# A hybrid inference step: weights of the first projection by column, top-k over halves, attention's units in another order

## What is computed

```python
def reference(...):
    for layer in range(2):
        mp = split(silu(c_ctx) @ mod_w[layer] + mod_b[layer], 6)     # context
        ms = split(silu(c) @ mod_w[layer] + mod_b[layer], 6)         # latent
        hp, hs = modulate(xp, norm1_g, mp[0], mp[1]), modulate(xs, norm1_g, ms[0], ms[1])
        if layer == 0:   # gate, u = x @ w_in; conv over 4; h_t = a_t h_(t-1) + b_t, both ways
            yp, ys = recurrent_mixer(hp, ...), recurrent_mixer(hs, ...)   # (h * gelu(gate)) @ w_out
        else:            # 16 heads of 64, 4 of keys; window of 128; sink; context keys for all
            yp, ys = context_attention(...) @ w_o, latent_attention(...) @ w_o
        xp, xs = xp + mp[2] * yp, xs + ms[2] * ys
        xp = xp + mp[5] * experts(modulate(xp, norm2_g, mp[3], mp[4]))
        xs = xs + ms[5] * experts(modulate(xs, norm2_g, ms[3], ms[4]))

def experts(x):
    aff = softmax(x @ w_router)                     # tokens x 16
    g, idx = top_k(aff.T, cap)                      # per expert, cap = tokens / 8
    h = silu(x[idx] @ w_gate) * (x[idx] @ w_up)
    return zeros.at[idx].add((h @ w_down) * g)
```

## Time and profile before

| | |
|---|---|
| median of 3 runs | 1864.85 us (1864.16 to 1870.14) |
| the profiled execution | 1864.11 us, its span 1862.3 us |
| PE busy | 1659.7 us, 89% of the span |
| DVE, ACT, POOL busy | 614.3, 370.4, 312.1 us |
| HBM read | 500.50 MB |

### The profile page before, as it was taken

The page is one execution under the profiler, slowest core; times in us unless marked ns, Lnnn a source line. Parts: engine busy times, 40 slices in busy tenths (PEclk is TensorE's granted clock), DMA queues, the critical chain, the costliest instruction groups (busy, mean ns, idle before and its releaser), DMA issues.

```text
span 1862.3 us, 30729 instructions
## 1 busy us (share of the span) xinstructions
PE 1659.7 (89%) x13351; PEld 771.2 (41%) x13351; DVE 614.3 (33%) x1137; ACT 370.4 (20%) x770; POOL 312.1 (17%) x358
## 2 busy tenths in 40 slices
PE   4799859479999999999879788794799999999997
PEld 0688647123333333332258666472233333333322
DVE  2467675510111121010267567556101111210102
ACT  2377741100000000000151355411000000000000
POOL 1133230210101110110020167301101011101110
PEclk8899979689999999999989899896899999999999
DMA  9400553989999999999920200315899999999993
GB/s 390 146 1 1 214 224 119 410 335 404 382 405 410 399 407 414 401 404 405 336 85 1 96 24 24 137 79 216 313 405 381 403 410 399 405 415 398 407 356 115
DMA packets 57934, 524.99 MB, mean 282 GB/s; under 512 B 12607, under 2 KB 12895, under 8 KB 25038
## 3 DMA queue, kind: packets, MB, share of 16 engines
q1 hardware_dynamic: 48096, 490.62, 64.9%
q0 software_dynamic: 8176, 27.08, 5.2%
q10 hardware_dynamic: 1534, 5.38, 0.7%
HBM read 500.50 MB, written 22.55 MB: 281 GB/s over the span
## 4 chain that ended last, share of the span: by engine, by line
PE 77%; DVE 9%; DMA 5%; ACT 5%; issue 2%; POOL 1%; SPq 0%; DVEq 0%; POOLq 0%; ACTq 0%
PE ps L912 36%; PE ps L916 18%; PE ps L855 6%; PE ps L1170 5%; DMA W<-x_hat,gi_c 2%; DMA ring<-in_mod_w 2%; DMA ring<-in_rg_w_in 1%; PE ps L1218 1%; PE ps L1192 1%; PE ps L1205 1%; PE ps L939 1%; PE ps L1077 1%; PE ps L954 1%; PE ps L759 1%; ACT W L1426 1%
## 5 line engine op out<-in xcount | busy, mean ns | idle before, releaser
L912 PE MATMUL ps<-ring,W 128*32 128x512 f32 x4608 | 552.4, 597 | 4.0 <-issue 2.6
L916 PE MATMUL ps<-ring,W 128*16 128x512 f32 x2304 | 300.2, 593 | 0.0
L912 PEld LDWEIGHTS ps<-ring,W 128*32 128x32 f32 x4608 | 145.9, 110 | 335.1 <-issue 333.0
L1241 ACT ACTIVATE W<-ps 128x512 f32<-128x512 f32 (+5 forms) x137 | 72.0, 542 | 910.5 <-PE ps L954 707.7
L1738 DVE TENSOR_TENSOR W<-ps,amod 128x1024 f32<-128x1024 f32 (+1 forms) x32 | 28.5, 892 | 487.4 <-PE ps L939 366.2
L912 PE MATMUL ps<-over_rows,W 128*32 128x512 f32 x1536 | 182.7, 593 | 0.0
L916 PEld LDWEIGHTS ps<-ring,W 128*16 128x16 f32 x2304 | 67.6, 97 | 177.3 <-issue 177.3
L1747 DVE TENSOR_TENSOR W<-ps,W 128x1024 f32<-128x1024 f32 x16 | 19.6, 1225 | 278.1 <-PE ps L916 278.1
L916 PE MATMUL ps<-over_rows,W 128*16 128x512 f32 x768 | 99.9, 592 | 0.0
L855 PE MATMUL ps<-wo_hl,mo_hi 128*128 128x512 f32 x320 | 89.7, 403 | 5.3 <-DVE mo_lo L1652 5.3
L912 PEld LDWEIGHTS ps<-over_rows,W 128*32 128x32 f32 x1536 | 48.1, 110 | 108.3 <-issue 107.8
(11 more groups left out here) (282 smaller groups left out, 2189.0 us busy)
## 6 DMA issues: line engine op xcount, KB each, us to landing
ring<-in_moe_w_down SPq DMA_DIRECT2D x52, 2048.0 KB, 11.7
ring<-in_moe_w_up SPq DMA_DIRECT2D x48, 2048.0 KB, 13.4
ring<-in_moe_w_gate SPq DMA_DIRECT2D x44, 2048.0 KB, 11.3
ring<-in_mod_w SPq DMA_DIRECT2D x48, 1024.0 KB, 11.3
over_rows<-in_moe_w_gate SPq DMA_DIRECT2D x20, 2048.0 KB, 11.1
over_rows<-in_moe_w_up SPq DMA_DIRECT2D x16, 2048.0 KB, 11.8
over_rows<-in_moe_w_down SPq DMA_DIRECT2D x12, 2048.0 KB, 12.9
ring<-in_rg_w_in SPq DMA_DIRECT2D x8, 1024.0 KB, 27.5
```

What stands on the lines that cost most here:

```text
L912: nc.tensor.matmul(ps[q * CG:(q + 1) * CG, bank + n, :], lat(q, k), expert_slots(slots[q // 2], 1)[:, 0, cols], start=(k == 0), stop=(k == ...
L916: mm = nc.tensor.matmul(ps[q * CG:q * CG + CC, bank + 2, :], ctx(a, k), expert_slots(slots[a], 1)[:, 0, h * D + n * 512:h * D + (n + 1) * ...
L1241: nc.scalar.activation(out, in_, ACT.Copy).then_inc(done, n)
```

## The change

- **Start.** The host lays `w_in` out by column blocks: slot b holds columns for block b of both halves and all input rows (`in_columns`). Only m0 and m1 are loaded before it and done before `turn(0)`; m2, m3 and m4 are loaded behind `w_in`, m2 and m3 computed behind the last projection, m4 where it was, and the three rows are turned together after m4. POOL's first two high parts stand ahead of its memset, and DVE's rest of column 0 stands inside the loop of `turn(0)`, behind block 4.
- **Weights behind the recurrence.** All eight rests of `w_out` are made by DVE, none by POOL; ACT makes all eight highs in a row, after row m4 and ahead of `mo_hi`.
- **Out-projection.** The 48 matmuls of a tile are parted: 32 with the weights' highs (`main_terms`), 16 with their rests (`weight_rests`). The order is main terms of tile 0, main terms of tile 1, rests of tile 0, gate rows, rests of tile 1, and from tile 2 on main terms and rests of each.
- **Top-k.** The latent tokens are laid out as two halves of 256 in rows 0 to 15 and 64 to 79, the context in rows 32 to 47, so that eight rounds run on 256 columns. Both halves give a sorted list of 64; one of them is written backwards and the better of each pair of entries is taken. `il` and `ic`, which the first gather needs, are written first, and POOL waits for those four only. A dummy exponential stands ahead of the wait for the logits.
- **Attention.** The eight context units stand behind every second four-block unit of j = 1 and 2, and j = 3 is last. POOL splits `w_o` in 32 quarters of 128 x 256, a cast and a subtraction in each unit from the third on.

A piece of a quarter's width stands behind every unit instead of a whole one behind every second, and a unit of one key block (2 x 128) stands between the large ones. The diff's core:

```diff
-MOD_SLOT = {0: 0, 1: 4, 2: 8, 3: 0, 4: 4, 5: 8, 6: 0, 7: 4, 9: 8, 10: 0, 8: 0, 11: 8}
-SLOT_LOADS = (("m0", "w_in", "m3", "m6", "moe0", "m10", "m8", "qkv", "moe1"),
-              ("m1", "w_in", "m4", "m7", "moe0", "qkv", "moe1"),
-              ("m2", "w_out", "m5", "moe0", "m9", "w_o", "m11", "moe1"),
+MOD_SLOT = {0: 8, 1: 4, 2: 0, 3: 4, 4: 0, 5: 8, 6: 0, 7: 4, 9: 8, 10: 0, 8: 0, 11: 8}
+SLOT_LOADS = (("w_in", "m2", "m4", "m6", "moe0", "m10", "m8", "qkv", "moe1"),
+              ("m1", "w_in", "m3", "m7", "moe0", "qkv", "moe1"),
+              ("m0", "w_out", "m5", "moe0", "m9", "w_o", "m11", "moe1"),
...
+        units = []
+        for j in range(TL):
+            for hp in range(KB):
+                units.append((j, hp))
+                if j in (1, 2) and hp % 2:
+                    units.append((TL, 4 * (j - 1) + hp // 2))
...
-            for v in range(3):
+            for v in range(2):
                 load_mod(v, None, None)
-            for s in range(KB):
-                sp.wait_ge(ring_used, used(s // 4, s))
-                put(s, rg_w_in[s * P:(s + 1) * P, :])
+            for b in range(4):
+                put(b, rg_w_in[b])
...
+            for b in range(4, KB):
+                sp.wait_ge(ring_used, used(1, b))
+                put(b, rg_w_in[b])
             for l in range(2):
                 sp.dma_start(router[:, l], moe_router[l].rearrange("(k p) e -> p k e", p=P)).then_inc(router_in, 16)
-            for v in (3, 4):
-                load_mod(v, wcol_lo_ok, lambda s: 2 * KB)
+            load_mod(2, wcol_lo_ok, lambda s: 2 * (s + 1))
+            load_mod(3, wcol_lo_ok, lambda s: 2 * (s + 5))
+            load_mod(4, ring_used, lambda s: used(2, s))
...
+            def column_high(n):
+                if n >= 2:
+                    pool.wait_ge((u_mm, g_mm)[n % 2], n // 2)
+                pool.wait_ge(slot_ready[n // 2], ready("w_in", n // 2))
+                nc.gpsimd.tensor_copy(wcol[n % 2][:, 0], in_columns(n)).then_inc(wcol_hi_ok, 1)
+            pool.wait_ge(ring_used, used(0, 3))
+            column_high(0)
+            column_high(1)
...
-            for k in range(KB // 2):
-                pool.wait_ge(wo_hi_ok, k + 1)
-                nc.gpsimd.tensor_tensor(wo_hl[:, k, 1, :], ring[:, KB + k // 2, (k % 2) * D:(k % 2 + 1) * D],
-                                        wo_hl[:, k, 0, :].bitcast(F32), ALU.subtract).then_inc(wo_lo_ok, 1)
-            for v in range(3, 5):
+            for v in range(2, 5):
...
-                pool.wait_ge(route_ok, 10 * (layer + 1))
+                pool.wait_ge(route_ok, 10 * layer + 4)
...
+                if u == 2:
+                    pool.wait_ge(qkv_mm, NT)
+                    for k in range(KB):
                         pool.wait_ge(slot_ready[KB + k // 2], ready("w_o", KB + k // 2))
-                        pool.wait_ge(qkv_mm, NT)
-                        nc.gpsimd.tensor_copy(wo_hl[:, k, 0, :], w).then_inc(wo_hi_ok, 1)
-                    else:
-                        pool.wait_ge(wo_hi_ok, KB + k + 1)
-                        nc.gpsimd.tensor_tensor(wo_hl[:, k, 1, :], w, wo_hl[:, k, 0, :].bitcast(F32), ALU.subtract).then_inc(wo_lo_ok, 1)
+                if 2 <= u < 4 * KB + 2:
+                    quarter_high(u - 2)
+                if 3 <= u < 4 * KB + 3:
+                    quarter_rest(u - 3)
...
+            def main_terms(layer, t, first):
+                toks = slice(t * P, (t + 1) * P)
+                for k in range(KB):
+                    if first:
+                        pe.wait_ge(wo_hi_ok, split_done(layer, k))
+                        for ok in (mo_hi_ok, mo_lo_ok):
+                            pe.wait_ge(ok, KB * layer + k + 1)
+                    for x in (mo_hi, mo_lo[layer]):
+                        for n in range(2):
+                            nc.tensor.matmul(ps[:, 2 * (t % 2) + n, :], x[:, k, toks], wo_hl[:, k, 0, n * 512:(n + 1) * 512],
+                                             start=(k == 0 and x is mo_hi), stop=False)
+            def weight_rests(layer, t, first):
+                toks = slice(t * P, (t + 1) * P)
+                for k in range(KB):
+                    if first:
+                        pe.wait_ge(wo_lo_ok, split_done(layer, k))
+                    for n in range(2):
+                        mm = nc.tensor.matmul(ps[:, 2 * (t % 2) + n, :], mo_hi[:, k, toks], wo_hl[:, k, 1, n * 512:(n + 1) * 512],
+                                              start=False, stop=(k == KB - 1))
+                mm.then_inc(out_mm, 1)
...
+                    if t == 0:
+                        for u in range(2):
+                            main_terms(layer, u, first=(u == 0))
+                        weight_rests(layer, 0, first=True)
+                    elif t == 1:
+                        weight_rests(layer, 1, first=False)
+                    else:
+                        main_terms(layer, t, first=False)
+                        weight_rests(layer, t, first=False)
...
+            modulation(0, 1)
+            pe.wait_ge(mod_read, 2)
...
+                    modulation(2, 3, turns=False, turn_last=False)
...
+                nc.scalar.activation(exp_row[:, layer:layer + 1], ones[0:1, 0:1], ACT.Exp)
...
-            out_weights_high(range(KB // 2))
             mod_reads([4])
+            out_weights_high(range(KB))
             mixed_high(0)
-            out_weights_high(range(KB // 2, KB))
...
+                for cols, ts in ((0, slice(0, 2)), (HB, slice(2, TL)), (32, slice(TL, NT))):
+                    n = ts.stop - ts.start
+                    v.tensor_tensor(aff[:, 0:n, cols:cols + NE], lg[:, ts], mx5[:, 1, ts].unsqueeze(2).to_broadcast([P, n, NE]),
+                                    ALU.mult).then_inc(aff_ok, 1)
...
+                both = tk[0:HB + NE, 0:NHALF]
+                step(v.tensor_copy(both, ps[0:HB + NE, 5, 0:NHALF]))
                 for r in range(CL // 8):
                     k8 = slice(8 * r, 8 * r + 8)
-                    step(v.max(tv[0:48, k8], tk[0:48, :]))
-                    step(v.max_index(ti[0:48, k8], tv[0:48, k8], tk[0:48, :]))
+                    step(v.max(tv[0:HB + NE, k8], both))
+                    step(v.max_index(ti[0:HB + NE, k8], tv[0:HB + NE, k8], both))
                     if r < CL // 8 - 1:
-                        step(v.match_replace(tk[0:48, :], tv[0:48, k8], tk[0:48, :], -1.0))
+                        step(v.match_replace(both, tv[0:HB + NE, k8], both, -1.0))
...
+                lists = ps[:, 4, 0:2 * (HB + NE)].rearrange("p (m n) -> p m n", m=2)
+                step(v.tensor_copy(merged[:, 0:2], lists[:, :, second]))
+                v.tensor_tensor(merged[:, 2], lists[:, 0, first], merged[:, 0], ALU.is_ge)
+                step(v.tensor_tensor(merged[:, 3], lists[:, 1, first], merged[:, 1], ALU.subtract))
+                v.tensor_tensor(merged[:, 0], lists[:, 0, first], merged[:, 0], ALU.max)
+                step(v.tensor_tensor(merged[:, 3], merged[:, 3], merged[:, 2], ALU.mult))
+                step(v.tensor_tensor(merged[:, 1], merged[:, 1], merged[:, 3], ALU.add))
+                pairs = [a.rearrange("p (e a) -> p e a", a=2) for a in (merged[:, 0], merged[:, 1], lists[:, 0, context], lists[:, 1, context])]
...
+                if b == KB // 2:
+                    column_rest(0)
```

151 lines of the change are left out of this document (70 added, 81 removed).

## The result

| | before | changed |
|---|---|---|
| median of the first runs | 1866.37 us (1864.16 to 1870.14, 4 runs) | 1850.78 us (1843.96 to 1853.82, 4 runs) |
| ratio | | 0.990, 95% interval 0.988 to 0.992 |
| profiled execution | 1864.11 us, span 1862.3 | 1843.96 us, span 1842.2 |
| timed again later | 1867.8 us (7 runs) | 1848.85 us (1846.99 to 1851.96) |

The change is faster, by 16 to 19 us in the medians and by 20 in the profiled executions. The forecast was 30 faster, 1834, with a range up to 1845: the median lies outside it. The four executions of the changed kernel lie 9.9 us apart; what this spread consists of is told with the first experiment.

A forecast was written before the change was run, and what follows sets the result against it. The prediction saw experts' matmuls (54 per cent of the span) keeping PE busy, so gains only where PE waits: -14.4 - 3.4 + 2.6 - 13.0 - 2.0 = -30.2 from 1864.11, forecast 1834 us, range 1823 to 1845.

The forecast's parts named there:

- Start, -14.4: Before the first projection of layer 0: fewer vectors ahead and no wait for w_in, 14.4 us gained; bounds -15.6 and -12.4.
- a rest that hides: Start's bound of -15.6 us: the rest of column 0 inside DVE's loop costs no time.
- End of the recurrent blocks, -3.4: Before layer 0's out-projection: DVE runs undisturbed by POOL, ACT is late next; 3.4 us gained, bounds -6.6 and 0.
- Out-projection, +1.3 each: Both layers: 1.8 us back from split-paced first tile, 3.0 stall behind gate rows; 1.3 lost each, bounds -1.8 and +3.2.
- Top-k, -6.5 each: Both layers: rounds on 256 instead of 512 columns, less added small steps; 6.5 us gained each, bounds -8 and -4.
- The table preload, nothing: Top-k's exponential: the table load already runs ahead of its operands, so preloading gains nothing; the dummy costs .15 us.
- Between the top-k and the attention, 0: First gather and experts: the gather's 13.54 us after issue and the experts' matmuls stay unchanged.
- Attention, -2: Layer 1's attention: interleaving and quarters -1, vector 11 -1.8, longer drain about 1; 2 us gained, bounds -8 and +6.
- Vector 11 at full clock: In attention: modulation's vector 11 follows three-block units where the clock is 1.00; 5.47 to 3.6 us, -1.8.
- rival 1: Attention loses: POOL's pieces and context units lengthen the loop, +6 instead of -2; 1842, or 1846 with half clock; chance .17.
- Rivals 3 to 6: Start not earlier, 1844 (.04); experts transfer-bound, 1847 (.04); preload gains, 1831 (.03); attention holds make it slower, 1872 (.03).
- rival 2: Attention gains more: context units cost the loop next to nothing, -8; 1828, or 1825 with the recurrent end's bounds; chance .12.

The follow-up runs named there:

- the first experiment: The changed kernel, unaltered, timed again beside the others: 1848.85 us (1846.99 to 1851.96), ratio to the kernel before 0.990.
- the second execution: The profiled execution of the unaltered changed kernel when timed again: span 1850.1 us, 7.9 more than its first profiled execution.
- vector 11: Gate rows early, context units last, quarters kept; modulation's vector 11 moved behind attention's last product, against the kernel without that move: 1828.89 us, ratio to before 0.979.

## Why the prediction was wrong, step by step

- **Start, -14.4.** Right; -15.6 in the trace, at the bound that I gave for a rest that hides. That is in part luck: the second vector was done .7 us earlier than before, .3 by its last piece's arrival and .4 by the clock, and the second execution kept only 13.6.
- **End of the recurrent blocks, -3.4.** Right in mechanism and near in size (-4.4): DVE undisturbed, ACT late next. The sum has a slip: 238.1 + .6 + 3.5 + 7.8 is 250.0 and not 249.6, which gives -3.0.
- **Out-projection, +1.3 each: the step that failed.** It measured +5.0 and +4.8. The stall was right, 3.15 for 3.0. Two things were not. "The first tile takes 12.73 against 10.90 for the next, since it is paced by splits" was a wrong reading: the excess was half clock behind the wait of 2.85 us in front of the tile, .50 in its first two microseconds, .64 in the next two and 1.00 after them, which makes 1.7 us, so the new order had nothing to give back. And the half clock behind the new stall, 1.6 us, I had seen, priced at 1.9 and put among the bounds and into a rival, though the row that gave the price stood behind waits of 2.28 and .51 us, shorter than this one. PE was done with both tiles and the gate rows 27.2 us after the start, against 27.1 before (I had 25.4). With both counted the term reads 0.1 + 3.15 + 1.6 = 4.9, within .2 of what was measured, and beyond the +3.2 that I gave as its bound. A wait of 3 us and its price in clock belong into one term. The two layers together are 7.2 of the 10.1 us missing in the profiled execution. Of the 16.8 us by which the median missed, these 7.2 are shown, and without them it would have been 1843.6, inside the range; 6.8 are the distance from that execution to the median.
- **Top-k, -6.5 each.** Right: -5.8 and -6.8, and .424 us for the maximum. The estimates for the small steps weren't tested one by one.
- **The table preload, nothing.** Right, .1 us lost.
- **Between the top-k and the attention, 0.** It measured +.8 at the first gather, which landed 14.30 us after its issue instead of 13.54. The first 96 expert matmuls took +2.2: .7 more wait for the second gather, the rest TensorE's clock after it. They took 22.25 to 24.5 us in the twelve traces of the changed kernel and its variants, so this differs between executions. Of the +1.8 up to the qkv projection 1.5 are the clock. Behind the same wait, before and then after:

```profile
935.67 1.07 PE L801 MATMUL ps<-ident,W 128*128 128x128 f32 x8 [1.54 <-ACT r L1267]
```

```profile
917.90 1.94 PE L823 MATMUL ps<-ident,W 128*128 128x128 f32 x8 [1.54 <-ACT r L1314]
```

  The vector of the modulation behind these transposes takes 4.23 instead of 3.61. It took 4.1 to 5.3 in all twelve traces and the stretch 45.1 to 46.8, against 43.5 in the one trace of before; whether the change brings the clock down there or that one execution was spared is open.
- **Attention, -2.** Right in sum (-1.9), wrong in parts. Vector 11 at full clock was right (5.47 to 3.62). For interleaving and quarters together I had -1; with the vector's share counted to the order they were -4 to -7 for the quarters and +4 to +7 for the order, and that these cancelled was luck. I held POOL's pieces in every unit against the quarters, while the row of the held operation spoke for them: a hold ends with POOL's piece, and the shorter pieces hold DVE shorter. And the price of a context unit among large ones had no row, only an estimate that left .6 us a round out.
- **The range.** Its upper end of 1845 took in rival 1 at 1842, whose mechanism, an attention 6 us longer, didn't happen, and left out its 1846 with the half clock of both out-projections, the one part of it that did. It took nothing in for the spread between executions: the sum was made against one profiled execution, .7 below a median of three, and that kernel's later medians were 1867.8 to 1869.6, so that execution was among its fastest. Held against the first profiled execution of the changed kernel, 1843.96, the range was just wide enough; against the median it was not.

Rivals 3 to 6 did not happen, nor did rival 2 as told: the first blocks of w_in came in time; behind the first 96 matmuls the experts took the same 514.9 us as before, in both layers of both first executions; the preload gained nothing; attention grew shorter, by 2 and not by 8.

## What to carry to other kernels

Before a term takes back what a tile "loses to pacing", look at how long its single instructions take: if all of a stretch are longer by a constant factor (1.05 against .62 us here) and the granted clock is down, it is the clock, and no new order of the same work gives it back. A piece of work that moves behind others moves all that waits for it; count the stall and the slower stretch behind it as one price, and try the place where the engine waits anyway, as vector 11 shows with 5 us. And two edits of one loop that cancel in a sum want two experiments, one each, since the better version keeps only one of them.

## What of the hardware I had not expected

- Twelve matmuls of no use in a stall of 3.15 us made the stretch 1.7 to 2.1 us shorter in each layer, 1.6 of it by keeping the granted clock at its upper level of 2.4 GHz in the tile behind it (7.30 instead of 8.59 us; the clock 1.00 instead of .84).
- The clock does not fall in the same places in every execution: at the three waits of 1.35, 1.21 and .69 us at the end of layer 0's experts it stayed at 1.00 in the changed kernel's first execution and was .92 over the stretch in the second. In 17 of 26 such places in the thirteen traces it fell, at a price of 1.3 to 3.0 us.
- An operation on 128 x 2 numbers, 160 ns long, had a mean of 255 to 494 ns in attention, by the size and place of another engine's pieces and the order of the units. Each held one ended with an instruction of that engine, and the longest took 2.24 us.
